# Four GpSimd instructions of 256 columns in place of one of 1024 for each weight slot's remainder

## The reference

```python
h = rmsnorm(x, norm_g)
(a_q, a_k, a_v, a_z, i_q, i_k, i_w, b_q, b_k, b_v, b_z, b_o, b_i, b_f, g_a, g_b) = split(h @ w_in)
# branch A: rope on a_q, a_k, i_q, i_k; index scores; top 128 keys of each query; softmax attention
score = einsum('th,ths->ts', w_i, relu(einsum('thd,sd->ths', q_i, k_i) / 8))
o_a = attention(q_a, k_a, v_a, keys in top_k(score, 128))
y_a = (o_a * silu(a_z)) @ w_branch_a
# branch B: causal convolution of width 4 on b_q, b_k, silu, a gated linear attention, head norm
qk_b = silu(causal_conv(concat(b_q, b_k), conv_w, conv_b))
y_b = (head_norm(sigmoid(b_o) * mlstm(qk_b, b_v, gates)) * silu(b_z)) @ w_branch_b
merged = sigmoid(g_a) * y_a + sigmoid(g_b) * y_b
out = rmsnorm(x + merged @ w_out, final_norm_g)
```

## Time and profile before

| what | value |
|---|---|
| median of 3 runs | 559.35 us (557.09, 559.35, 560.69) |
| span of the profiled execution, first to last instruction | 558.9 us |
| busy share of PE, DVE, ACT, POOL | 94%, 56%, 43%, 35% |
| POOL's remainders in the profile | 72, 2.4 us each |

### The profile page before, as it was taken

One profiled execution on the slowest core, in us unless ns is written; L12 is line 12 of the kernel. 1 busy time (PEld: TensorE's weight loads), 2 busy tenths in 40 slices (PEclk: granted clock), 3 DMA queues, 4 the chain that ended last, 5 costly groups with the idle time before them and its releaser, 6 DMA issues.

```text
span 558.9 us, 6744 instructions
## 1 busy us (share of the span) xinstructions
PE 525.9 (94%) x2488; PEld 427.7 (77%) x2488; DVE 311.2 (56%) x608; ACT 239.1 (43%) x414; POOL 194.1 (35%) x111
## 2 busy tenths in 40 slices
PE   4967999979999899999999999999999999998996
PEld 3656788867788687778777677888888888887885
DVE  3668489989999995432966858631111110125232
ACT  6833565525453345335555443414323212334222
POOL 0654133321433354414232222215544445553000
PEclk9988799989999989999999999999999999999999
DMA  8533121212222234112221111114222445515112
GB/s 263 187 114 114 39 75 39 75 43 72 76 75 76 84 101 136 39 38 77 75 76 38 39 32 44 39 39 113 76 75 75 114 113 147 186 62 208 39 38 76
DMA packets 44257, 47.89 MB, mean 86 GB/s; under 512 B 4928, under 2 KB 29632, under 8 KB 44224
## 3 DMA queue, kind: packets, MB, share of 16 engines
q1 hardware_dynamic: 43360, 46.33, 27.2%
q10 hardware_dynamic: 864, 1.12, 0.6%
HBM read 45.35 MB, written 2.10 MB: 85 GB/s over the span
## 4 chain that ended last, share of the span: by engine, by line
PE 69%; DVE 21%; ACT 4%; issue 4%; POOL 1%; DMA 1%; POOLq 0%; DVEq 0%; ACTq 0%
PE pj L1336 16%; PE pj L1337 15%; PE pj L1338 15%; DVE conv_acc L1096 4%; DVE score L1074 3%; PE ob L1444 2%; DVE score L1087 2%; DVE cell L1237 2%; DVE top L1086 2%; PE qb L1409 2%; PE ob L1418 2%; PE qb L1433 1%; PE tr L1438 1%; PE qb L1337 1%; PE qb L1336 1%
## 5 line engine op out<-in xcount | busy, mean ns | idle before, releaser
L500 POOL TENSOR_TENSOR w_lo<-w_raw,w_hi 128x1024 fp32r<-128x1024 f32 x71 | 170.9, 2417 | 202.6 <-ACT w_hi L775 202.6
L1336 PE MATMUL pj<-w_hi,h_hi 128*128 128x512 f32 x272 | 118.5, 436 | 2.0 <-POOL w_lo L500 2.0
L1337 PE MATMUL pj<-w_lo,h_hi 128*128 128x512 f32 x272 | 109.0, 401 | 0.0
L1338 PE MATMUL pj<-w_hi,h_lo 128*128 128x512 f32 x272 | 108.8, 400 | 0.0
L1336 PE MATMUL pj<-h_hi,w_hi 128*128 128x512 f32 (+1 forms) x200 | 78.2, 391 | 1.8 <-DVE h_lo L999 1.8
L775 ACT ACTIVATE w_hi<-w_raw 128x1024 fp32r<-128x1024 f32 (+1 forms) x74 | 75.7, 1047 | 8.8 <-DMA w_raw<-in_w_out 6.4
L1338 PE MATMUL pj<-h_hi,w_lo 128*128 128x512 f32 (+1 forms) x200 | 77.9, 389 | 0.0
L1337 PE MATMUL pj<-h_lo,w_hi 128*128 128x512 f32 (+1 forms) x200 | 77.8, 389 | 0.0
L1336 PEld LDWEIGHTS pj<-w_hi,h_hi 128*128 128x128 f32 x272 | 52.8, 194 | 16.1 <-issue 3.3
L1338 PEld LDWEIGHTS pj<-w_hi,h_lo 128*128 128x128 f32 x272 | 52.6, 193 | 12.2
L1337 PEld LDWEIGHTS pj<-w_lo,h_hi 128*128 128x128 f32 x272 | 53.0, 195 | 9.6 <-issue 1.0
(11 more groups left out here) (199 smaller groups left out, 833.0 us busy)
## 6 DMA issues: line engine op xcount, KB each, us to landing
w_raw<-in_w_in SPq DMA_DIRECT2D x60, 512.0 KB, 3.5
w_raw<-in_w_out SPq DMA_DIRECT2D x5, 512.0 KB, 3.7
x_tok<-in_x SPq DMA_DIRECT2D x4, 512.0 KB, 5.1
w_raw<-in_w_branch_a SPq DMA_DIRECT2D x8, 256.0 KB, 2.9
w_raw<-in_w_branch_b SPq DMA_DIRECT2D x8, 256.0 KB, 3.5
x_again<-in_x SPq DMA_DIRECT2D x1, 2048.0 KB, 10.1
w_late<-in_w_out SPq DMA_DIRECT2D x3, 512.0 KB, 7.2
out<-y_norm SPq DMA_DIRECT2D x4, 256.0 KB, 2.1
```

What stands on the lines that cost most here:

```text
L500: eng.tensor_tensor(lo[:, 0:m], raw_slot(n)[:, 0:m], hi[:, 0:m].bitcast(F32), ALU.subtract).then_inc(lo_by_dve if n in DVE_SLOTS else lo_b ...
L1336: pe.matmul(bank, a_hi, b_hi, start=first, stop=False)
L1337: pe.matmul(bank, a_hi, b_lo, start=False, stop=False)
L1338: return pe.matmul(bank, a_lo, b_hi, start=False, stop=last)
```

## The change

Where POOL makes a remainder, it now issues four instructions of 256 columns, one after the other, in place of one of 1024. Each counts `lo_by_pool`, and `wait_lo` waits for four times as many counts, so PE and SP still wait for the whole slot. The slots of DVE keep their one instruction. Nothing else is changed: the order on POOL, the ring, the places and the work of the other engines.

```diff
+PIECES = 4
...
-                eng.wait_ge(lo_by_pool, sum(1 for m in range(n + 1) if m not in DVE_SLOTS))
+                eng.wait_ge(lo_by_pool, PIECES * sum(1 for m in range(n + 1) if m not in DVE_SLOTS))
...
-            eng.tensor_tensor(lo[:, 0:m], raw_slot(n)[:, 0:m], hi[:, 0:m].bitcast(F32), ALU.subtract).then_inc(lo_by_dve if n in DVE_SLOTS else lo_by_pool, 1)
+            if n in DVE_SLOTS:
+                eng.tensor_tensor(lo[:, 0:m], raw_slot(n)[:, 0:m], hi[:, 0:m].bitcast(F32), ALU.subtract)\
+                    .then_inc(lo_by_dve, 1)
+                return
+            for a in range(0, m, m // PIECES):
+                cols = slice(a, a + m // PIECES)
+                eng.tensor_tensor(lo[:, cols], raw_slot(n)[:, cols], hi[:, cols].bitcast(F32), ALU.subtract)\
+                    .then_inc(lo_by_pool, 1)
```

## The result

The changed kernel takes 540.88 us (median of 4, 540.48 to 541.05) against 560.02 for the kernel before in the same comparison: a ratio of 0.9667, 95% interval 0.9640 to 0.9695, that is 19 us. Its profiled execution has a span of 539.0 us and a time of 540.72.

A forecast was written before the change was run, and what follows sets the result against it. PE, busy 94%, is the bound; it pays for DVE standing until one POOL instruction ends. Terms -3.6 - 3.7 - 3.4 - 0.6 - 3.6 + 0.9 = -14.0 on span 558.9 give 544.9, median 545.3 us; range 541 to 559.

The forecast's parts named there:

- the third rival: Clock stays up throughout: whole 4.4 us gained behind PE's 3.14 us wait, small late waits shrink; 541 or under; chance 0.06.
- 53.09: PE's 3.14 us wait for `rotate` at 53.09 us falls to 1.6, half of 4.4 us clock loss gained: -3.7 us.
- a slot of four pieces alone: POOL's time for one slot in four pieces: 3.0 us, 0.6 us more than one instruction.
- 35.66, with the start: PE's 4.47 us wait for `rotate` at 35.66 us falls to some 1 us; start costs +1.4; with clock, together -3.6 us.
- 116.42: PE's 2.86 us wait for `rotate` at 116.42 us falls to about 1, with 1.5 us of clock: -3.4 us.
- 133 and 147.72: PE's waits of 0.73 and 1.27 us for `rotate` at these times shrink by 0.25 and 0.35 us: -0.6.
- 193.96: PE's 2.04 us wait for a weight slot at 193.96 us vanishes: -2.0 us, and -1.6 of clock.
- waits behind 250 us: No gain in the sum; 2 us from small waits behind 300 us only if the clock stays up throughout, chance 0.06.
- the end: `w_out` slots from 495.14 us end later, delaying loads, ACT and `m_lo` ahead of 514.31: +0.9 us, between 0 and +2.0.
- The rival of taking turns: DVE pays a whole piece for each chained step, a triple loses 2.2 us as now: -1.4, 557.9 us; chance 0.22.
- Closing up: POOL lets no DVE step in between pieces, each stand of DVE grows with the slot: +6.3, 565.7 us; chance 0.10.
- a new wait for `w_lo`: Sign that the prediction is wrong: PE shows new waits for `w_lo`; no size given.

The follow-up runs named there:

- the second profile: The kernel before, unchanged, profiled once more: span 556.7 us, time 558.47 us.
- the runs by place: Changed kernel with four pieces for slots 5 to 28 alone, one instruction elsewhere: 543.38 us (0.9724); the reverse: 555.97 us (0.9960).

## Why the prediction was right, and where it was too small

The mechanism held. DVE stands still until POOL's instruction ends, it gets in between pieces, PE's waits shrink and the clock stays up. The forecast was -14.0 us, the measured difference -19.1 of the medians and -19.9 of the profiles. In size it is the third rival that came, the clock that stays up throughout, to which I had given 0.06: both of its conditions hold, the whole 4.4 us at 53.09 and the smaller waits behind 300 us, and 540.88 lies at its "541 or a little under", 0.1 us below the lower end of my range. Term by term, by the rows above:

| term | forecast | measured |
|---|---|---|
| a slot of four pieces alone | 3.0 us | 2.80 (16 pieces in 11.18 us at the start) |
| 35.66, with the start | -3.6 | -2.0 and clock -1.5: -3.5 |
| 53.09 | -3.7 | -1.7 and clock -4.4: -6.1 |
| 116.42 | -3.4 | -2.3 and clock -1.5: -3.8 |
| 133 and 147.72 | -0.6 | +0.2 - 0.3: -0.1 |
| a sixth wait for `rotate`, at 88.61 | 0 | +0.2 |
| 193.96 | -3.6 | -2.0 and clock -1.6: -3.6 |
| waits behind 250 us | 0 | -2.0 |
| the end | +0.9 | +0.2 |

Two terms make most of the miss. The first is the sentence "I take half of the 4.4 us of clock as gained". The wait left at this place is 1.43 us, not 1.6, and no clock is lost behind it, as behind the 1.27 of before. The 4.4 was itself a high value: the second profile has 1.5 behind a wait of the same length. I had read a price from one execution as if it were the kernel's. From the same execution came the span, 558.9, that I set 0.45 us under the median; with its time at some 560.7 the forecast of -14.0 would have been a time of 546.7.

The second is the zero for the waits behind 250 us. I put 2 us for them only into the case in which the clock stays up; they are in fact a third place of the same mechanism, on DVE's way to `probs`, and the runs by place show it. There the steps that scale `cell` stand still, which my reading of the rows, with both inputs from SBUF, had left out. What I did look for in the late slots, a price at the end, was 0.2 instead of 0.9.

At 35.66 the term came out right by luck. The transposes came at 33.68, as I had said (33.6), but the start cost 0.7 us and not 1.4, so PE's wait was 1.81 us and not 1. That is over the 1.27 which I took as the longest wait known to leave the clock up, and close to the 2.04 that cost 1.6; that the clock stayed up all the same, I had no row for.

Of the signs that I named, the steps of `rotate` at 31 us (0.37 to 0.71 us), the slot with DVE among its pieces (4.18), the waits for `rotate` (5.95) and the clock (1.00) came as stated; the six `conv` triples beside POOL took 2.7 to 3.6 us, four of them about 3.1, where I had counted 3.7. Of the signs of being wrong one appeared, a new wait for `w_lo`, but of 0.67 us and at the end alone, where I had looked for a price.

The rival of taking turns was right in its form and wrong in its price. The steps do alternate with the pieces, but I charged a whole piece, 0.75 us, for a turn. It costs 0.36 to 0.44, because a step doesn't meet the whole piece: the one at 31.40 starts 0.17 us into its piece, and its last 0.22 us, what it takes alone, begin 0.13 us before the piece's recorded end. With two pieces the form shows in full: four turns of some 1 us each eat the gain at that place.

Closing up did not happen; at 31 us a DVE step ended behind one piece after the other. The Trainium skill, "GPSIMD Engine Reference", section "Instruction dispatch", says that a core of this engine starts its next instruction without waiting for the other cores. The pieces do follow each other every 0.70 us, but what I drew from that rule, that there would be no gap for DVE, is refuted by the steps at 31.40 to 33.53 us.

The rule under which the change works at `rotate` and `conv` is that of "SBUF — State Buffer", section "Who interferes with whom" in the Trainium skill: a DVE instruction with two inputs in SBUF contends with a GpSimd instruction that reads SBUF, and whoever comes first holds the shared ports for its whole instruction. The trace agrees in both directions: `rotate` sits out POOL's piece (0.66 instead of 0.22 us), and a piece sits out a `conv` step (1.19 instead of 0.74).

Not settled: the 1.3 us that no wait names, and why the same wait is followed by 1.5 us of lost clock in one execution and by 4.4 in another.

## What to carry to other kernels

If an instruction of an engine with time to spare keeps an engine on the critical path standing, as POOL's did with DVE here, the length of the single instruction is the price, not the engine's busy time: cut it, and pay more busy time where nothing waits for its end. Count the chained steps on the other side, since each can meet a piece: at `rotate` two pieces against four steps gave next to nothing (5.0 us for 5.1), four pieces halved it (2.5), eight took it to 1.9. And cut by place: eight pieces were best where DVE was late, but cost 5.4 us of waits where slots stand in a row ahead of PE, and sixteen made POOL the pace.

## What the hardware showed that I had not expected

Matmuls that nobody needs made the kernel before 1% faster, by keeping the granted clock at 1.00 through three waits. The clock behind a wait of 3.1 us was 0.74 from 50 to 70 us in one execution and 0.91 in another of the same kernel. And POOL's subtraction follows a simple line: start to start, 0.70 us for 256 columns and 2.35 for 1024, that is 2.15 ns a column and 0.15 us; the 0.42 us of 128 columns (32 pieces in 13.40 us at the start, in the kernel with eight) lie on it. DVE's steps that scale `cell` stood still beside it although they read one tile only.
